# A two-layer hybrid decoder trunk in fp32: the projections that end a sublayer give their results by tokens instead of by features

## What is computed

```python
x = x + rmsnorm(f(rmsnorm(x, g_pre)), g_post)
```

## Time and profile before

| | |
|---|---|
| times of three executions | 931.27, 933.71, 935.31 us (median 933.71) |
| span of the profiled execution, first to last instruction | 935.2 us |
| PE, weight loads, DVE, ACT, POOL busy | 95%, 93%, 68%, 50%, 19% of the span |
| granted TensorE clock, mean over the span | 0.990 of 2.4 GHz |
| chain that ended last | PE 66%, DVE 21%, ACT 6%, POOL 2%, DMA 2% |
| read from memory | 151.58 MB, 163 GB/s |

### The profile page before, as it was taken

How to read it: one execution, slowest core, us unless ns; L and a number is a source line. 1 busy time by engine, 2 the same in 40 slices (tenths; PEclk the granted TensorE clock), 3 DMA queues, 4 the chain that set the end, 5 groups by cost and what they waited for, 6 DMA issues and landing times.

```text
span 935.2 us, 17320 instructions
## 1 busy us (share of the span) xinstructions
PE 890.5 (95%) x7354; PEld 866.8 (93%) x7354; DVE 638.7 (68%) x1006; ACT 468.9 (50%) x663; POOL 173.9 (19%) x165
## 2 busy tenths in 40 slices
PE   8899998999999999999989998999998799999996
PEld 7899998998989999999889988899998799999996
DVE  4686996687497555554779999855884675555552
ACT  6664554565465444444543333365653554444443
POOL 1120800000001000000048778655000010000000
PEclk9999999999999999999999999999999899999999
DMA  8454434544555656655645665444632355655551
GB/s 297 130 179 135 136 122 149 181 136 142 166 178 177 198 183 192 190 184 178 199 127 178 196 183 181 136 160 156 194 122 90 115 180 186 191 185 181 185 176 46
DMA packets 82821, 154.92 MB, mean 166 GB/s; under 512 B 6822, under 2 KB 8760, under 8 KB 82744
## 3 DMA queue, kind: packets, MB, share of 16 engines
q1 hardware_dynamic: 82632, 153.77, 52.3%
q10 hardware_dynamic: 112, 0.05, 0.0%
HBM read 151.58 MB, written 1.05 MB: 163 GB/s over the span
## 4 chain that ended last, share of the span: by engine, by line
PE 66%; DVE 21%; ACT 6%; POOL 2%; issue 2%; DMA 2%; DVEq 0%; SPq 0%; POOLq 0%; ACTq 0%
PE ps L556 20%; PE ps L557 20%; PE ps L558 20%; DVE w_lo L1420 8%; ACT w_hi L1036 3%; DVE ps L1765 2%; DMA raw<-in_ab_w_in 2%; POOL w_lo L2050 2%; DVE tmp L1703 1%; DVE h_lo L1431 1%; DVE xc L1487 1%; DVE xT L1710 1%; PE ps L778 1%; DVE cv L1938 1%; PE ps L918 1%
## 5 line engine op out<-in xcount | busy, mean ns | idle before, releaser
L1036 ACT ACTIVATE w_hi<-raw 128x1024 fp32r<-128x1024 f32 x284 | 295.2, 1054 | 231.4 <-DMA raw<-in_mlp_w 130.7
L1420 DVE TENSOR_TENSOR w_lo<-raw,w_hi 128x1024 fp32r<-128x1024 f32 x238 | 290.7, 1244 | 141.0 <-ACT w_hi L1036 137.0
L556 PE MATMUL ps<-h_hi,w_hi 128*128 128x256 f32 x1248 | 353.0, 283 | 20.8 <-DVE w_lo L1420 11.3
L557 PE MATMUL ps<-h_lo,w_hi 128*128 128x256 f32 x1248 | 349.9, 280 | 0.0
L558 PE MATMUL ps<-h_hi,w_lo 128*128 128x256 f32 x1248 | 349.8, 280 | 0.0
L556 PEld LDWEIGHTS ps<-h_hi,w_hi 128*128 128x128 f32 x1248 | 238.5, 191 | 25.2 <-DVE w_lo L1420 12.4
L558 PEld LDWEIGHTS ps<-h_hi,w_lo 128*128 128x128 f32 x1248 | 237.1, 190 | 0.0
L557 PEld LDWEIGHTS ps<-h_lo,w_hi 128*128 128x128 f32 x1248 | 236.8, 190 | 0.1
L556 PE MATMUL ps<-r_hi,w_hi 128*128 128x256 f32 x512 | 144.3, 282 | 0.0
L558 PE MATMUL ps<-r_hi,w_lo 128*128 128x256 f32 x512 | 144.1, 281 | 0.0
L557 PE MATMUL ps<-r_lo,w_hi 128*128 128x256 f32 x512 | 144.1, 281 | 0.0
(11 more groups left out here) (269 smaller groups left out, 1252.4 us busy)
## 6 DMA issues: line engine op xcount, KB each, us to landing
raw<-in_mlp_w SPq DMA_DIRECT2D x128, 512.0 KB, 3.8
raw<-in_cd_w_in SPq DMA_DIRECT2D x40, 512.0 KB, 3.9
raw<-in_xa_wkv SPq DMA_DIRECT2D x32, 512.0 KB, 3.8
raw<-in_ab_w_in SPq DMA_DIRECT2D x24, 512.0 KB, 4.5
raw<-in_xa_wq SPq DMA_DIRECT2D x16, 512.0 KB, 4.0
raw<-in_xa_wo SPq DMA_DIRECT2D x16, 512.0 KB, 3.8
raw<-in_cd_w_out SPq DMA_DIRECT2D x16, 512.0 KB, 3.9
raw<-in_ab_w_out SPq DMA_DIRECT2D x12, 512.0 KB, 3.7
```

The source lines that it names most:

```text
L556: nc.tensor.matmul(dst, wt[0], x[0], start=start, stop=False, skip_group_check=True)
L557: nc.tensor.matmul(dst, wt[0], x[1], start=False, stop=False, skip_group_check=True)
L1036: nc.scalar.activation(w_hi[:, v % SLOTS, :, :], raw[:, v % SLOTS, :, :], ACT.Copy)\
L1420: V.tensor_tensor(w_lo[:, v % SLOTS, :, :], raw[:, v % SLOTS, :, :], f(w_hi[:, v % SLOTS, :, :]), ALU.subtract).then_inc(lo_ready_dve, 1)
```

## The change

out, wo and w2 of both layers are made by a new function `tokens` instead of `project`: the activations are stationary and 512 weight columns move, as in `v_group`. The result m[2g + t] is a bank with 128 tokens (tile t) on partitions and the 512 features of half g. All that follows changes with it:

- The sum of squares is now along the free axis: ACT's square gives it as an accumulated sum (`ssq`), with no partition sums on the PE and no spreading of factors. DVE makes the mean in two small steps for each token tile (left half g = 0, then right half), POOL the power for each tile.
- ACT scales the left half of m with the tile's factor into `mt`, DVE the right half. The PE turns `mt` back with 16 transposes into four banks `mT`, after the first filler unit, and runs the other three filler units behind them.
- DVE makes new x in one step from `mT`: gain x mT + xT. `tmp` is no longer there.
- The order of w_lo and w_hi among these steps is another, and the factor after the MLP is made by DVE in one more step instead of by three on POOL.
- At the end, the gain comes as a row spread over the partitions (`gpost`, a new load), DVE multiplies by it (`mg`), nothing is transposed behind the last matmul, and the stores go by token tile.
- Banks: the sets no longer differ by layer, and four banks for `mT` are named at each boundary. In SBUF `ssq` and a skip of 2304 bytes take the place of `tmp` (2048 bytes) and a skip of 352.

The diff, cut to its core (bank names, calls that only change their name, and the two-unit tail of `tokens` are left out):

```diff
@@ sync: the loop over units, and the stores @@
+                if u == first[("w1", 1, 2)]:
+                    sp_.dma_start(gpost[:, :], A["norm_gains"][1, 5:6, :].broadcast_to([P, D])).then_inc(gpost_landed, 16)
...
-                hf, t = i // 2, i % 2
+                t, hf = i // 2, i % 2
@@ tensor @@
+            def tokens(seg, dest, src, k0=0, first_k=True, last_k=True, ready=None, only=None, tail=2):
+                def products(u, i, t, kt, start, stop):
+                    hi, lo = (x[:, t * P:(t + 1) * P] for x in src(kt))
+                    wh, wl = w_hi[:, u % SLOTS, i, :], w_lo[:, u % SLOTS, i, :]
+                    dst = bank(dest[t])
+                    nc.tensor.matmul(dst, hi, wh, start=start, stop=False)
+                    nc.tensor.matmul(dst, hi, wl, start=False, stop=False)
+                    return nc.tensor.matmul(dst, lo, wh, start=False, stop=stop)
...
             def boundary(l, n, filler):
                 filler([0])
-                pe.wait_ge(dve_made, after("dve", "S2", l, n))
-                token_sums(("nstat", l, n), halves(S2))
-                filler([1])
-                pe.wait_ge(pool_made, after("pool", "nr", l, n))
-                rows(("nrow", l, n), [rfac[:, 1 + 3 * l + n, t:t + 1] for t in range(TT)])
-                filler([2, 3])
+                for i in range(4):
+                    if i == 0:
+                        pe.wait_ge(act_made, after("act", "mt", l, n, 1))
+                    if i == 2:
+                        pe.wait_ge(dve_made, after("dve", "mt", l, n, 1))
+                    transposes(("mT", l, n, i), [((c * TT + t) * P, mt[:, t, (2 * i + c) * P:(2 * i + c + 1) * P], P)
+                                                 for c in range(2) for t in range(TT)])
+                filler([1, 2, 3])
@@ scalar @@
+                def squares(n, m, i):
+                    act.wait_ge(*full(m[i]))
...
+                    nc.scalar.activation(sq[:, i % 2, :], bank(m[i]), ACT.Square, accum_out=ssq[:, 3 * l + n, i:i + 1])\
+                        .then_inc(act_made, tick("act", "nsq", l, n, i))
+                def normed(n, m, t):
+                    act.wait_ge(pool_made, after("pool", "nr", l, n, t))
+                    nc.scalar.activation(mt[:, t, 0:512], bank(m[t]), ACT.Copy, scale=rfac[:, 1 + 3 * l + n, t:t + 1])\
+                        .then_inc(act_made, tick("act", "mt", l, n, t))
...
                     round_to(x + 1)
+                    squares(n, m, 0)
+                    squares(n, m, 1)
+                    round_to(x + 2)
+                    squares(n, m, 2)
+                    normed(n, m, 0)
+                    squares(n, m, 3)
                     round_to(x + 3)
+                    normed(n, m, 1)
+                    new_h(tag, gl, gs, nxt)
+                    round_to(nxt + 5)
@@ vector @@
-            def new_x(l, n, m, tag, gl, gs, lows):
+            def new_x(l, n, tag, gl, gs, lows):
...
-                        V.scalar_tensor_tensor(out=tmp[:, j % 2, :], in0=bank2(m[j // 2])[:, j % 2, :],
-                                               scalar=gain(l, 2 * n + 1, j), in1=Nrow[:, :], op0=ALU.mult,
-                                               op1=ALU.mult).then_inc(dve_made, tick("dve", "dx", l, n, j))
+                        if j % 2 == 0:
+                            dve.wait_ge(*full(("mT", l, n, j // 2)))
+                        V.scalar_tensor_tensor(out=xT[:, j, :], in0=bank2(("mT", l, n, j // 2))[:, j % 2, :],
+                                               scalar=gain(l, 2 * n + 1, j), in1=xT[:, j, :], op0=ALU.mult,
+                                               op1=ALU.add).then_inc(dve_made, tick("dve", "x", tag, j))
...
-                low_to(x if fill else x + 1)
-                norm_sum(l, n, m)
-                if fill:
-                    low_to(x + 1)
-                factor(l, n)
-                dve.wait_ge(pool_made, after("pool", "nr", l, n))
-                low_to(nxt + 1)
-                new_x(l, n, m, tag, gl, gs, {3: nxt + 2, 6: nxt + 3})
-                low_to(nxt + 4)
+                low_to(x)
+                norm_left(l, n, 0)
+                norm_left(l, n, 1)
+                low_to(x + 1)
+                norm_right(l, n, 0)
+                normed(l, n, m, 0)
+                norm_right(l, n, 1)
+                low_to(x + 2)
+                normed(l, n, m, 1)
+                new_x(l, n, tag, gl, gs, {1: x + 3, 3: nxt, 5: nxt + 1})
+                low_to(nxt + 3)
...
+            dve.wait_ge(gpost_landed, 16)
+            for t in range(TT):
+                norm_left(1, 2, t)
+                weighted(t)
+            for t in range(TT):
+                norm_right(1, 2, t)
+                weighted(2 + t)
+                dve.wait_ge(pool_made, after("pool", "nr", 1, 2, t))
...
```

More of the change, by code:

```diff
@@ L306, in trunk @@
         mhalf = sb("mhalf", [8])
-        tmp = sb("tmp", [2, T])
-        skip(352)
+        ssq = sb("ssq", [6, 4])
+        skip(2304)
         with ExitStack() as s:
@@ L361, in trunk @@
             otok = sb("otok", [TT, D], scope=s)
-            mg = sb("mg", [J, T], scope=s)
+            mg = sb("mg", [TT, D], scope=s)
+        with ExitStack() as s:
+            skip(42432, s)
+            mt = sb("mt", [TT, D], scope=s)
+            gpost = sb("gpost", [D], scope=s)
         ps = ctx.enter_context(nc.psum_tensor("ps", [P, 8, 512], F32))
@@ L901, in _ @@
                 if l == 0:
-                    project(("out", 0, "early", 0), out_banks(0, 0), mix0, k0=ke, last_k=False,
+                    tokens(("out", 0, "early", 0), out_banks(0, 0), mix0, k0=ke, last_k=False,
                             ready=mix_ready(0))
@@ L932, in _ @@
                     token_sums(("varstat",), halves(S2))
-                    project(("out", 1, "early", 1), out_banks(1, 1), mix1, k0=ke, last_k=False, only=[3])
+                    tokens(("out", 1, "early", 1), out_banks(1, 1), mix1, k0=ke, last_k=False, only=[3])
                     pe.wait_ge(pool_made, after("pool", "lnr"))
@@ L963, in wo @@
                     k0 = 0 if part == "early" else 4
-                    project(("wo", l, part, g), [("wo", l, g, 0), ("wo", l, g, 1)], h_src, k0=k0,
-                            first_k=part == "early", last_k=part == "late", only=only,
-                            ready=lambda kt: pe.wait_ge(dve_made, after("dve", "o", l, kt // 2)))
+                    tokens(("wo", l, part, g), [("wo", l, g, 0), ("wo", l, g, 1)], h_src, k0=k0,
+                           first_k=part == "early", last_k=part == "late", only=only,
+                           ready=lambda kt: pe.wait_ge(dve_made, after("dve", "o", l, kt // 2)))
                 if l == 0:
@@ L1017, in _ @@
                 w2(7, (g,))
-            for g in range(2):
-                pe.wait_ge(act_made, after("act", "mg", 4 * g + 3))
-                for t in range(TT):
-                    transposes(("mout", g, t), [(q * P, mg[:, 4 * g + q, t * P:(t + 1) * P], P) for q in range(4)])
-                if g == 0:
-                    pe.wait_ge(dve_made, after("dve", "S2", 1, 2))
-                    token_sums(("nstat", 1, 2), halves(S2))
         @block.scalar
@@ new lines, in norm_right, with normed @@
+                V.scalar_tensor_tensor(out=stat[:, s_, t:t + 1], in0=ssq[:, 3 * l + n, 2 + t:3 + t], scalar=1.0 / D,
+                                       in1=stat[:, s_, 2 + t:3 + t], op0=ALU.mult, op1=ALU.add)\
+                    .then_inc(dve_made, tick("dve", "nv", l, n, t))
+            def normed(l, n, m, t):
+                dve.wait_ge(pool_made, after("pool", "nr", l, n, t))
+                V.tensor_scalar(mt[:, t, 512:1024], bank(m[2 + t]), rfac[:, 1 + 3 * l + n, t:t + 1], None, ALU.mult)\
+                    .then_inc(dve_made, tick("dve", "mt", l, n, t))
+                freed("dve", m[2 + t])
@@ L2175, in _, with norm_rsqrt @@
                     low_to(F_[("K", 1, 1)] - 1)
-                pool.wait_ge(dve_made, after("dve", "nv", l, 0))
-                rsqrt(rfac[:, 1 + 3 * l, 0:2], stat[:, 1 + 3 * l, 0:2], "nr", l, 0)
+                def norm_rsqrt(n):
+                    for t in range(TT):
+                        s_ = 1 + 3 * l + n
+                        pool.wait_ge(dve_made, after("dve", "nv", l, n, t))
+                        rsqrt(rfac[:, s_, t:t + 1], stat[:, s_, t:t + 1], "nr", l, n, t)
+                norm_rsqrt(0)
                 low_to(F_[("q", l, 0)] + 3)
```

259 lines of the change are left out of this document (121 added, 138 removed).

## The result

The changed kernel takes 924.94 us (median of four executions, 924.30 to 927.24) where the kernel before takes 933.72 (931.27 to 935.31): ratio 0.9917 [0.9897, 0.9937], 8.8 us. The sign is right and the time lies in the range, at its upper edge, but less than half of the forecast 18.6 us came.

What follows compares the result with a forecast made beforehand. PE, busy 95% of the span, bounds the kernel: matmul pace and waits. Terms -7.2 - 2.8 - 2.8 - 2.1 - 3.7 = -18.6 us from 933.7 give 915 us; forecast 911 to 920 (chance 0.58), eight-in-ten range 906 to 925.

Steps and rivals of the forecast that it cites:

- w2: MLP's second projection: 2.85 us per unit falls to 2.74 at 228 ns, 0.11 saved on 64 units, -7.2 us.
- a rival with 925 us: w2 and out keep 237 to 242 ns per long matmul; only boundaries and end gain: 925 us, chance 0.14.
- w1: MLP's first projection, untouched by the change: 113.4 ns per 128x256 matmul in layer 0, no term in the sum.
- Behind the gate: No term of its own; the four w_lo (4 x 1.22) between factor and new x at filled boundaries are spread out.
- Filled boundaries: Four sublayer boundaries with V or K filler: 3.8 us added, 6.6 of stalls gained, -2.8 us; transposes ready E+2.7 to E+3.0.
- The stalls of the next projections: q of layer 0, w1, gate and q of layer 1 behind filled boundaries stop stalling: all 6.6 us counted as gained.
- Turned results come late: Rival: at filled boundaries ACT scales 2 us late, four boundaries lose 8 us, stalls stay: 923 to 929 us, chance 0.08.
- out: Mixers' output projections in both layers, early and late units, at 228 ns per long matmul: together -2.8 us.
- Unfilled boundary: wo to w1 in layer 1, without filler: 7.44 us falls to 5.3, -2.1 us.
- end: Last matmul to kernel end: 10.08 us falls to 6.4, -3.7 us.
- Both ends: Clock loss of some 1.9 us in layer 1's first w1 group: change of 0 or -1.9; left as is.
- wo and attention: wo at 113.5 against 114 ns per 256 columns: 0 us; no term for the attention around it.

Runs made afterwards that it cites:

- edit 1: Changed kernel, but at the boundary after layer 0's MLP DVE subtracts the first unit of a before its sums of new x: 922.23 us, 0.9850.
- Edits 1, 2 and 8: Changed kernel plus a's first subtraction before the gate's sums, DVE's scaling before the subtraction beside POOL's power, r 64 bytes further: 911.60 us, 0.9747.
- the fastest version: Changed kernel with a's first subtraction and DVE's scaling both moved earlier and r moved by 64 bytes, no added joint matmul: 911.60 us, 0.9747.

## Why the prediction was half right

- **w2: the step that failed.** "I take 228, because moving tile and shape are those of the earlier trace rows and only the stationary one differs." The stationary one was what mattered: with r where it lies, 232 ns (11.13 us for 48). Put h in its place, or move r by 64 bytes, and it is 229. So w2 won some 4.2 us in place of 7.2, and w1 took half of that back. The prediction had the clue: it saw that h, r and mixer operands differ in pace, and made of it a rival with 925 us. That rival's time came out, but by luck: it needed 237 to 242 ns, and much of the rest was lost at the gate and the fillers, which it left alone.
- **w1: a term that was missing.** The sum held w1 at 113.4 ns, since nothing in it changes. But the earlier trace rows show only layer 0; in layer 1 the same w1 groups took 11.31 us before, at the same clock (the line below). A pace that differs between two runs of the same code is not the shape's, and can move when its neighbour does. It took 2.5 us back in layer 0 (6 x 0.42) and gave 0.4 in layer 1.

```profile
775.79:787.10 11.31, 11.31 (x99) 11.31 (x97) 4.65 (x5) 4.55 (x5) 0.00 (x0) 1.00 0.48 151
```

- **Behind the gate: costed at nothing, cost 2.95.** "The four w_lo (4 x 1.22) that stood between factor and new x are spread out." Not one of these four but the last of the row, which used to follow new x (nxt + 4, at the gate the first unit of `a`), came to stand behind the sums, and so behind a wait of 5.06 us on DVE, with the PE's next unit queued behind it. The clock at 0.50 that followed cost little on top: the mixer stage is 0.74 us longer than before, and with edit 1, without that fall, it is longer still. The prediction counted how many subtractions stood ahead of new x, but not which unit each belongs to and who waits for the last.
- **Filled boundaries: right chain, wrong link.** E+2.7 to 3.0 us was forecast for the transposes, E+3.4 measured. The whole difference is POOL's power, 1.47 beside DVE's subtraction where 0.70 was taken. The fillers so cost +5.7 and not +3.8. The stalls of the next projections went as forecast: -6.0 of -6.6, the rest because q 0, w1 and gate run at 117.8 ns. "Turned results come late" was a rival with ACT as the cause; it was POOL, and 0.66 us, not 2.
- **out:** -1.7 of -2.8. The early units moved as forecast (11.62 to 11.06), but the long matmuls run at 230 ns, and the late groups still wait for the mixer's chain (25.16 to 24.79).
- **Unfilled boundary: sum right, by luck; end: right.** The stretch took 6.27 us where 5.3 was forecast, since the power is the slow one here too (1.46). The first w1, which was left as it was, lost 1.7 us less to the clock: 0.50 at the transposes, back 1.0 us into w1. The two misses offset each other. Both ends had been named for the clock, 0 and -1.9, and the wrong one was taken. The end took 5.88 us, 6.4 forecast (its terms add up to 6.5).
- **wo and attention:** the -1.9 us in layer 1 was not forecast. 1.6 of it lies in the stretch from the first turned probabilities to the end of the scores (5.60 to 4.03 us); what makes them earlier was not tried.

Edits 1, 2 and 8 win back 13.3 us by the medians (924.94 - 911.60), more than the 9.9 between forecast and result. So the three causes can cover the shortfall, but the two sums are not of the same things. Some 2.0 of the 13.3 are w1 groups of layer 1 that the kernel before had slow as well (5 x 0.40), and the profile of the fastest version has the clock at 0.50 neither behind the gate (6.8 us as changed) nor at the unfilled boundary (3.4). The better end, unfilled boundary and attention had hidden part of the shortfall.

## What to carry to other kernels

When a PE-bound loop's pace changes though its code did not, compare the same code in two places of the trace first: here, two paces for one shape came from the place of an operand and from the joint with the neighbour, and moving a tile by 64 bytes is a cheap test. In a row of minimum, median and maximum, ask where the maximum comes from, above all for an engine that shares something with another. When an order of work is rewritten, write down for each moved instruction the unit it serves and the wait that now stands ahead of it.

## What was not expected of the hardware

- The place of an operand in SBUF changed the PE's pace: with r 64 bytes further, w2 goes from 231.9 to 228.8 ns per long matmul and w1, which doesn't read it, from 117.8 to 113.6. Why this place is better is open: one other place was tried.
- The same 128x256 matmuls have two steady paces at full clock, and kept the one that they started with to the end of their group. In the slow one a third of the stationary loads take 4 ns more. Loads of line 558, third of the three products, in the w1 group at 299 us, as changed and with r moved:

```profile
L558 PEld LDWEIGHTS ps<-h_hi,w_lo x28: 192/192/193, 299.0 to 308.6; 128*128 128x128 f32 x28
```
```profile
L558 PEld LDWEIGHTS ps<-h_hi,w_lo x30: 187/188/188, 298.8 to 308.7; 128*128 128x128 f32 x30
```

- One matmul of 64 columns, 0.03 us, at the joint moved 96 others from the slow to the fast pace. In layer 0 it also moved one group (w1's second) the other way, from 10.99 to 11.39 us.
